# All four gated branches of a transformer mixer in one stage, with the convolution's norm done in steps inside its jobs

## What is computed

```python
def _conformer_conv(u, dw, dw_bias, ln_g, ln_b):
    a, g = jnp.split(u, 2, axis=-1)
    v = a * jax.nn.sigmoid(g)
    y = lax.conv_general_dilated(v, dw[:, None, :], window_strides=(1,),
        padding=[(15, 15)], feature_group_count=384, ...) + dw_bias     # 31 taps
    return jax.nn.silu(_layer_norm(y, ln_g, ln_b))                       # over 384 features

    g_f, g_d, g_g, g_c = jnp.split(jax.nn.sigmoid(gate_logits), 4, axis=-1)   # gate_logits = h @ w
    merged = (g_f * (y_f @ w_br_fourier) + g_d * (o_d @ w_br_diff)
              + g_g * (o_g @ w_br_gqa) + g_c * (y_c @ w_br_conv))
    return merged @ w_out
```

## Time and profile before

| | |
|---|---|
| median of 3 runs | 4546.71 us (4542.3 to 4547.37) |
| the profiled execution | 4543.03 us |
| its span in the profile, first to last instruction | 4541.1 us |
| mean granted TensorE clock | 0.928 |
| TensorE busy | 3841.5 us, 85% |
| VectorE, ScalarE, POOL busy | 35%, 18%, 22% |
| layer 0: gates, conv_norm, gates_conv, first matmul of each | from 1905.7; from 2264.9; from 2288.3 to the output stage at 2403.2 |
| layer 1: the same | from 3694.3; from 3925.4; from 3944.8 to the output stage at 4019.8 |

### The profile page before, as it was taken

How to read it: one execution, slowest core, us unless ns; L and a number is a source line. 1 busy time by engine, 2 the same in 40 slices (tenths; PEclk the granted TensorE clock), 3 DMA queues, 4 the chain that set the end, 5 groups by cost and what they waited for, 6 DMA issues and landing times. The chain is left out here.

```text
span 4541.1 us, 46402 instructions
## 1 busy us (share of the span) xinstructions
PE 3841.5 (85%) x18182; PEld 2615.0 (58%) x18182; DVE 1578.6 (35%) x2861; ACT 839.9 (18%) x1723; POOL 1009.8 (22%) x782
## 2 busy tenths in 40 slices
PE   6967838777669968799988799998797889888997
PEld 5865625444455536555555355555584657666886
DVE  2355320000031168444422423323215834424334
ACT  2123210000030135311121200001202521111001
POOL 1300200000003220122232222222042023334442
PEclk8978959889879979999999899999898999998999
DMA  4420239999711100022211122321020012121221
GB/s 184 194 99 15 93 148 392 398 397 401 287 51 55 57 1 1 27 91 92 85 70 65 56 107 98 112 93 56 28 75 24 1 48 81 64 87 56 84 88 52
DMA packets 80996, 500.85 MB, mean 110 GB/s; under 512 B 9824, under 2 KB 11278, under 8 KB 27022
## 3 DMA queue, kind: packets, MB, share of 16 engines
q1 hardware_dynamic: 71406, 475.86, 27.8%
q0 software_dynamic: 4112, 13.11, 0.9%
q10 hardware_dynamic: 5264, 8.92, 0.5%
HBM read 476.86 MB, written 20.99 MB: 110 GB/s over the span
## 5 line engine op out<-in xcount | busy, mean ns | idle before, releaser
L1726 PE MATMUL ps<-expert_weights,experts_x_turned 128*64 128x256 f32 x2048 | 273.6, 427 | 88.0 <-DMA expert_weights<-w_moe 87.0
L1726 PEld LDWEIGHTS ps<-expert_weights,experts_x_turned 128*64 128x64 f32 x2048 | 189.3, 155 | 182.4 <-issue 136.5
L548 PE MATMUL ps<-projected,weight_ring 128*128 128x384 f32 (+1 forms) x672 | 245.9, 522 | 0.0
L548 PEld LDWEIGHTS ps<-projected,weight_ring 128*128 128x128 f32 x672 | 127.9, 190 | 105.9 <-issue 45.9
L1852 DVE TENSOR_TENSOR experts_hidden<-experts_silu_gate,ps 128x256 f32<-128x256 f32 x32 | 13.5, 422 | 482.3 <-PE ps L1726 482.3
L2578 PE MATMUL ps<-h2b,weight_ring 128*128 128x384 f32 (+1 forms) x512 | 154.1, 446 | 23.7 <-PEq L237 23.7
L2082 PE MATMUL ps<-h2b,weight_ring 128*128 128x384 f32 (+1 forms) x512 | 154.0, 445 | 15.4 <-PEq L237 15.4
L812 PE MATMUL ps<-projected 64*128 64x256 f32 (+1 forms) x576 | 121.3, 538 | 54.0 <-ACT attention_prob L875 49.7
L2172 DVE SCALAR_TENSOR_TENSOR projected<-projected,sb_vectors 128x497 f32<-128x497 f32 (+26 forms) x270 | 157.8, 650 | 1.3
L2558 POOL TENSOR_TENSOR mlp_weight_sums<-weight_ring 128x512 f32<-128x512 f32 x32 | 43.0, 1344 | 472.0 <-DMA weight_ring<-w_stream 331.5
L906 DVE TENSOR_REDUCE attention_shift<-ps 128x1 f32<-128x768 f32 (+1 forms) x160 | 128.7, 846 | 32.6 <-PE ps L812 31.0
(11 more groups left out here) (672 smaller groups left out, 7625.3 us busy)
## 6 DMA issues: line engine op xcount, KB each, us to landing
weight_ring<-w_stream SPq DMA_DIRECT2D x218, 1024.0 KB, 5.0
expert_weights<-w_moe SPq DMA_DIRECT2D x198, 1024.0 KB, 27.6
slot_out<-experts_down_out ACTq DMA_DIRECT2D x64, 128.0 KB, 7.4
weight_ring<-w_stream SPq DMA_DIRECT2D x16, 512.0 KB, 3.6
slot_out<-sb_constants SPq DMA_DIRECT2D x15, 512.0 KB, 5.1
weight_ring<-w_stream SPq DMA_DIRECT2D x16, 384.0 KB, 3.2
sb_x_all<-xT SPq DMA_DIRECT2D x1, 3072.0 KB, 12.4
tokens<-h_tokens SPq DMA_DIRECT2D x1, 2048.0 KB, 6.6
```

Source lines behind the costliest of these rows:

```text
L548: ins = nc.tensor.matmul(core.ps[:, 2 * slot + half, 0:n], w_of(k), h_of(k)[:, a:a + n], start=(first and k == 0), stop=(last and k == chu ...
L1726: ins = nc.tensor.matmul(out[OWN * j:OWN * (j + 1), :], x_t[:, k, :], w[j][:, k, :], start=(k == 0), stop=(k == KD - 1), skip_group_check= ...
```

## The change

The two calls of `gates_phase` and the call of `conv_norm_phase` between them become one call with all four branches, 16 jobs, and 16 modulation units in layer 0. `conv_norm_phase` is gone. The taps are spread over the first 9 jobs (`TAPPED = 9`; 3, 3, 4, 3, 4, 3, 4, 3, 4 a job). The norm is done in steps:

- job 9: TensorE sums the chunks, one half of the columns after product 2 and the other after product 5 (`statistic`), both into bank 3, which the modulation uses too, so it waits for `bg.added` first, and for `tapped`, which VectorE signals by a small memset behind the last tap. VectorE makes the mean of each half between its adds and subtracts it where the taps were; ScalarE squares after its sigmoids.
- job 10: the same two statistics of the squares; ScalarE takes Ln of each half between its other work, and Exp after its sigmoids.
- job 11: VectorE scales, ScalarE takes Silu.
- jobs 12 to 15 are the convolution branch; TensorE waits for `normed` ahead of its branch part.

Mean and reciprocal root lie in two chunks of the first branch's input, and the squares in the convolution's old input.

```diff
-def gates_phase(core, name, layer, h, pr, merged, branches, first_branch, span, conv, mods=()):
+def gates_phase(core, name, layer, h, pr, merged, branches, span, mods=()):
...
+    TAPPED = 9
...
+        mean, rstd = [pr[:, branches[0][0] + i, a:a + cols] for i in range(2)]
+        tapped, stat_done, mean_out, centred, sq_ready, ln_ready, rstd_ready, scaled, normed = [ph.sem(x) for x in (
+            "tapped", "statistics_done", "mean_out", "centred", "squares_ready", "ln_ready", "rstd_ready",
+            "conv_scaled", "conv_normed")]
...
+                def statistic(src, i):
+                    for c in range(3):
+                        ins = nc.tensor.matmul(ps[:, 3, 0:n], core.ones[:, :], half(src + c, i), start=(c == 0),
+                                               stop=(c == 2), skip_group_check=True)
+                        stream.note(ins)
+                    ins.then_inc(stat_done, 1)
...
                 product(z, s[:, 0], right(0, 1), True, False)
+                if j == TAPPED:
+                    if bg:
+                        pe.wait_ge(bg.added, bg.n_turn)
+                    pe.wait_ge(tapped, 1)
+                    statistic(acc, 0)
+                if j == TAPPED + 1:
+                    if bg:
+                        pe.wait_ge(bg.added, bg.n_turn)
+                    pe.wait_ge(sq_ready, 3)
+                    statistic(val, 0)
...
                 product(y, s[:, 2], th[:, 1], False, False)
+                if j == TAPPED:
+                    pe.wait_ge(mean_out, 1)
+                    statistic(acc, 1)
+                if j == TAPPED + 1:
+                    pe.wait_ge(ln_ready, 1)
+                    statistic(val, 1)
...
+                if b == len(branches) - 1:
+                    pe.wait_ge(normed, 3)
...
+                if j == TAPPED:
+                    pe.wait_ge(mean_out, 2)
+                if j == TAPPED + 1:
+                    pe.wait_ge(ln_ready, 2)
                 if bg:
                     bg.rows(pe)
...
+            def ln(i):
+                act.wait_ge(stat_done, 3 + i)
+                nc.scalar.activation(rstd[:, i * n:(i + 1) * n], ps[:, 3, 0:n], ACT.Ln, bias=core.eps(),
+                                     scale=1.0 / (3 * P)).then_inc(ln_ready, 1)
...
                 nc.scalar.activation(quarter(1, 1), z, ACT.Copy).then_inc(m5_out, 1)
+                if j == TAPPED + 1:
+                    ln(0)
...
                 nc.scalar.activation(quarter(1, 1), quarter(1, 1), ACT.Sigmoid).then_inc(sig_ready, 1)
+                if j == TAPPED + 1:
+                    ln(1)
...
                 nc.scalar.activation(quarter(1, 0), quarter(1, 0), ACT.Sigmoid).then_inc(sig_ready, 1)
+                if j == TAPPED:
+                    for c in range(3):
+                        act.wait_ge(centred, c + 1)
+                        nc.scalar.activation(pr[:, val + c, a:a + cols], pr[:, acc + c, a:a + cols], ACT.Square) \
+                            .then_inc(sq_ready, 1)
+                if j == TAPPED + 1:
+                    act.wait_ge(ln_ready, 2)
+                    nc.scalar.activation(rstd[:, :], rstd[:, :], ACT.Exp, scale=-0.5).then_inc(rstd_ready, 1)
+                if j == TAPPED + 2:
+                    for c in range(3):
+                        act.wait_ge(scaled, c + 1)
+                        nc.scalar.activation(pr[:, acc + c, a:a + cols], pr[:, acc + c, a:a + cols], ACT.Silu,
+                                             bias=core.v(f"ln_b{layer}", c)).then_inc(normed, 1)
...
+            def mean_half(i):
+                dve.wait_ge(stat_done, i + 1)
+                nc.vector.tensor_scalar(mean[:, i * n:(i + 1) * n], ps[:, 3, 0:n], 1.0 / (3 * P), None, ALU.mult) \
+                    .then_inc(mean_out, 1)
...
                 nc.vector.tensor_tensor(quarter(0, 1), y, quarter(1, 0), ALU.add).then_inc(u2_out, 1)
+                if j == TAPPED:
+                    mean_half(0)
...
                 nc.vector.tensor_tensor(quarter(1, 1), y, quarter(1, 1), ALU.add).then_inc(c22_out, 1)
+                if j == TAPPED:
+                    mean_half(1)
...
-                while conv and tap < CONV2 * (j + 1) // len(jobs):
+                while tap < min(CONV2, CONV2 * (j + 1) // TAPPED):
                     conv_tap(tap)
                     tap += 1
+                if j == TAPPED - 1:
+                    nc.vector.memset(mean[:, 0:1], 0.0).then_inc(tapped, 1)
+                if j == TAPPED:
+                    dve.wait_ge(mean_out, 2)
+                    for c in range(3):
+                        nc.vector.tensor_tensor(pr[:, acc + c, a:a + cols], pr[:, acc + c, a:a + cols], mean[:, :],
+                                                ALU.subtract).then_inc(centred, 1)
+                if j == TAPPED + 2:
+                    dve.wait_ge(rstd_ready, 1)
+                    for c in range(3):
+                        nc.vector.scalar_tensor_tensor(pr[:, acc + c, a:a + cols], pr[:, acc + c, a:a + cols],
+                                                       core.v(f"ln_g{layer}", c), rstd[:, :], ALU.mult, ALU.mult) \
+                            .then_inc(scaled, 1)
                 dve.wait_ge(sig_ready, 4 * j + 4)
...
-def conv_norm_phase(core, layer, pr, span):
...
                 gates_phase(core, f"gates{layer}", layer, h, pr, merged,
-                            [(DQ, 4), (GQ, 4), (UF, 3)], True, span, True,
-                            () if last else mod_units("mod0", 8, 20))
-                conv_norm_phase(core, layer, pr, span)
-                gates_phase(core, f"gates_conv{layer}", layer, h, pr, merged, [(UC + 3, 3)],
-                            False, span, False, () if last else mod_units("mod0", 20, 24))
+                            [(DQ, 4), (GQ, 4), (UF, 3), (UC + 3, 3)], span, () if last else mod_units("mod0", 8, 24))
```

77 lines of the change are left out of this document (11 added, 66 removed).

## The result

| | before | after |
|---|---|---|
| median | 4546.86 us (4542.3 to 4547.37, 4 runs) | 4500.55 us (4498.9 to 4503.66, 4 runs) |
| ratio | | 0.9901, 95% interval 0.9884 to 0.9918 |
| profiled execution, its span | 4543.03, 4541.1 us | 4503.66, 4501.8 us |
| gating stages, layer 0 and layer 1 | 497.50 and 325.53 us | 475.09 and 302.89 us |

The change is faster by 46.3 us, 1.0%, against 46.7 forecast. The last line runs from the first matmul of the gates to the first matmul of the output stage. It fell by 22.41 and 22.64 us, 45.05 together.

The account below looks back on a forecast made before the run. TensorE's record streaming was taken to bound the gating stages, with one idle seam per layer. Savings of 22.9 and 21.9 us, 44.8 together, off 4543.03 gave 4498.2, said as 4500; own range 4495 to 4510, at 83%.

Parts of the forecast that it names:

- The seam: Between the two gating stages: removing the wait and slow first job saves 32.64 us in layer 0, 28.30 in layer 1.
- Statistics: Ones-matmuls on TensorE in the merged stage, fully on the path: 7.74 us added in layer 0, 5.19 in layer 1.
- Stall: Job 9's first statistic waits for taps and, in layer 0, VectorE's modulation add: 1.4 us, layer 1 0.6.
- Taps forward at nothing: 31 taps in 9 jobs instead of 12, 3 or 4 a job, cost nothing beyond the stall.
- ScalarE's table loads at nothing: Norm's Ln, Exp and Silu between sigmoids: 8 loads per layer instead of 4, 1.28 us each, hidden, costing nothing.
- POOL's later start: Nine more semaphores to clear on POOL ahead of the output stage, 0.065 us each: 0.6 us per layer.
- time given back in the output stage beyond 0.6 us: Output stage: one of the listed signs that would show the forecast wrong.
- The sum: Layer 0 22.9 and layer 1 21.9, together 44.8 us off the profiled 4543.03: 4498.2, median said as 4500.
- (a): Rival: norm's chain through ScalarE is on the path in jobs 10 and 11; 16 loads exposed, 20.5 us, 4519; 10%.
- (b): Rival: VectorE bounds the first nine jobs, with 31 taps instead of 23; 42.1 us if all exposed, 4540; 3%.
- (c): Rival: seam's wait only moves to the convolution branch, whose matmuls wait for normed input; 12.6 us back, 4511; 2%.
- (d): Rival: waits before statistics drop TensorE's clock to half in jobs 9 to 11; 147 us more, 4645, slower; 2%.

## Why the prediction was right, and where its terms were off

- **The seam, 32.64 and 28.30 us.** Right. The stage times account for it: 60.94 less the statistics (7.73 and 5.20), the stalls (1.10 and 0.46) and the chance half clock of job 0 (1.39) is 45.06, and 45.05 were measured.
- **Statistics, 7.74 and 5.19 us.** Right to 0.01. They lie fully on the path in layer 0, as the kernel without the norm shows. In layer 1 their net cost is 1.24 us less, since without them product 4 would wait for that long.
- **Stall, 1.4 and 0.6 us.** 1.10 and 0.46. The mechanism was right, the modulation add behind four taps. The memset took 0.06 us and not 0.15, which is part of it; TensorE stood still for 0.84 us of the 1.10, and the statistic behind ran 2.20 us instead of 2.10.
- **Taps forward at nothing.** Right for 9 jobs and for 8: every job but job 0 of layer 0 and those with statistics kept its length to 0.01 us. At 6 it would have failed, most in layer 1, where the prediction had counted the least slack.
- **ScalarE's table loads at nothing.** Right; taking them all away changed the stages by 0.01 us. The rows of the kernel after show 1.28 us a load with nothing behind it but the activation. The price of the Trainium skill (ScalarE: Activation LUTs, What ACT_TABLE_LOAD costs), about 2.66 us with a drain, finds support in them for the load and none for the drain: the load at 2218.45 begins 0.02 us after the activation before it ends.
- **POOL's later start, 0.6 us per layer.** The start was right (0.57) and its effect was not: the term should have been 1.79 and 1.25 us at the third product, and, with the half clock of the third, 1.78 and 2.07 at the fourth. The step that failed took TensorE's wait to grow by POOL's delay, without asking what POOL's sums run beside. The prediction had named time given back in the output stage beyond 0.6 us as a sign of being wrong, and in this term it was. The hint was in the trace of before: POOL's first sum of a stage took 1.55 us in one stage and 2.38 in another.
- **The sum** of 44.8 us against the 46.3 by medians is closer than its parts. From profile to profile the time fell by only 39.4 us: the gating stages gave 45.05, 2.1 were lost ahead of layer 0's gates, where no instruction changed, and 3.6 behind the gating stages, where the prediction had 1.2. The output stages were longer by 1.79 and 2.94 us up to the first matmul of the squares (L438); the matmuls of the squares, more of which ran at half clock before, gave some of that back. The profiled execution was the slowest of the four of the kernel after, and that of the kernel before lay 3.8 us under its median. So a part of the closeness is luck of a few microseconds, within what runs of one kernel differ by.
- **Rivals.** (a) refuted by the kernel without table switches; (b) not reached, but real at 6 jobs in layer 1; (c) refuted by the kernel without the norm, whose convolution jobs were as long; (d) refuted: the clock was 1.00 in jobs 9 to 11, and even after a wait of 4.73 us only the half of a statistic right behind it ran below that. One argument against (d) was misread, though: it said that in the steady jobs seven products with waits between them run at 1.00, and the rows show no waits there (27.45 us busy of 27.45). What the Trainium skill (TensorE: Matmul & The Clock Gate, A second HAM failure mode: psum-queue depth-cycling) tells of short idles between groups and a swinging clock did not come about in these stages. TensorE stands still three times in a gating stage of the kernel after, 0.13, 2.62 and 0.84 us in layer 0, and the half clock behind the 2.62 us was over within job 0.

## What to carry to other kernels

A chain of small operations between two stages costs its whole length with the matmul engine mostly idle, and some more in the slow first job behind it; and the stage's end makes the matmul engine wait for the last job's work on the other engines. Cut into steps and laid between the matmuls of a full stage it costs only its own matmuls, so ask of each step who waits for it there (table loads cost nothing, the last tap 1 us) and let the idle engines shrink those matmuls (three chunks added first, 8 us more). When such a change lengthens something at the next stage's start, don't carry the delay over one to one: look at which two engines run side by side there, since half a microsecond cost a whole turn of 1.79 us here.

## What the runs showed of the hardware

- POOL's weight sums and VectorE's column sums, additions and subtractions of two fp32 operands in SBUF, take turns operation by operation. Beside VectorE's column sums POOL's first sums took 2.76 to 2.78 us each in layer 0, alone 1.26. With the column sums gone, the fourth product of the output stage started 5.06 us earlier in layer 0 and 3.48 in layer 1; of this 1.8 and 0.8 us are the third product's, which then ran at full clock.
- After the end of layer 0's gates one or two products run wholly or for the most part at half clock, in the twelve profiles at different ones of the output stage's first three. It costs 1.4 to 1.7 us where the product is the one that is waited for, and nothing where a wait follows that absorbs it. The third product took 4.28 to 4.54 us in six of the twelve and 2.74 to 2.85 in the others. Up to 1.7 us of what two profiles differ by can be this alone. In job 0 of layer 1's gates the third and fourth product ran partly at half clock in eleven of the twelve profiles, and that job then took 24.1 us and not 22.4.
